# Level differences of three gated recurrences: from the vector engine to GpSimd

## What is computed

```
# gla_mixer (4 heads, dk 64), hgrn2_scan (8 heads, dk 128); b = cumsum(log of the gate)
decay = exp(b[t] - b[s])            for s <= t, else 0
attn  = einsum('td,sd,tsd->ts', q, k, decay)
o     = attn @ v   (+ what the earlier chunks carry in)
```

```
q[t]·k[s]·exp(b[t]-b[s]) = (q[t]·exp(b[t]-b[m])) · (k[s]·exp(-(b[s]-b[m])))     m = the last token of the first half
```

## Time and profile before

| | us |
|---|---|
| median of 3 runs | 1308.67 |
| lowest, highest | 1304.14, 1310.24 |
| the profiled execution, its own time | 1304.06 |
| its span, first to last instruction | 1302.2 |
| PE busy in the span | 1213.9 |
| DVE busy | 794.1 |
| ACT busy | 590.8 |
| POOL busy | 0.2 |

### The profile page before, as it was taken

One profiled execution on the slowest core, in us unless ns is written; L12 is line 12 of the kernel. 1 busy time (PEld: TensorE's weight loads), 2 busy tenths in 40 slices (PEclk: granted clock), 3 DMA queues, 4 the chain that ended last, 5 costly groups with the idle time before them and its releaser, 6 DMA issues. The chain is left out here.

```text
span 1302.2 us, 22187 instructions
## 1 busy us (share of the span) xinstructions
PE 1213.9 (93%) x9296; PEld 1146.4 (88%) x9296; DVE 794.1 (61%) x963; ACT 590.8 (45%) x706; POOL 0.2 (0%) x4
## 2 busy tenths in 40 slices
PE   5999999987999997998988899999999998999997
PEld 4988889987999996898888788888888797999997
DVE  3466666757555556358879544863444665777775
ACT  3553445344443444366444434544333444554553
POOL 0000000000000000000000000000000000000000
PEclk8999899998999998999998899899999899999999
DMA  6522433542555552253222233342333253554540
GB/s 245 194 98 98 162 130 130 195 162 69 190 183 175 190 183 76 79 213 112 102 91 86 98 130 117 110 162 98 130 129 130 97 199 129 184 177 185 190 164 33
DMA packets 26507, 183.14 MB, mean 141 GB/s; under 512 B 3120, under 2 KB 3776, under 8 KB 4544
## 3 DMA queue, kind: packets, MB, share of 16 engines
q1 hardware_dynamic: 26432, 182.04, 39.3%
HBM read 180.98 MB, written 1.05 MB: 140 GB/s over the span
## 5 line engine op out<-in xcount | busy, mean ns | idle before, releaser
L271 DVE TENSOR_TENSOR wlo<-raw,whi 128x2048 fp32r<-128x2048 f32 x170 | 389.4, 2291 | 260.5 <-ACT whi L264 256.9
L276 PE MATMUL pp<-XH,whi 128*128 128x256 f32 x1792 | 516.7, 288 | 11.8 <-DVE HF L811 9.3
L276 PE MATMUL pp<-XL,whi 128*128 128x256 f32 x1792 | 511.5, 285 | 0.0
L276 PE MATMUL pp<-XH,wlo 128*128 128x256 f32 x1792 | 511.2, 285 | 0.0
L276 PEld LDWEIGHTS pp<-XH,whi 128*128 128x128 f32 x1792 | 348.4, 194 | 21.8 <-DVE HF L811 10.6
L264 ACT ACTIVATE whi<-raw 128x2048 fp32r<-128x2048 f32 x170 | 324.0, 1907 | 83.6 <-PE pp L276 61.0
L276 PEld LDWEIGHTS pp<-XL,whi 128*128 128x128 f32 x1792 | 348.7, 195 | 0.0
L276 PEld LDWEIGHTS pp<-XH,wlo 128*128 128x128 f32 x1792 | 348.4, 194 | 0.0
L1326 PE MATMUL pm<-Y,whi 128*128 128x256 f32 x640 | 116.1, 283 | 0.0
L1326 PEld LDWEIGHTS pm<-Y,whi 128*128 128x128 f32 x640 | 99.8, 192 | 0.0
L1326 PE MATMUL pm<-Y,wlo 128*128 128x256 f32 x320 | 90.6, 283 | 0.0
(11 more groups left out here) (278 smaller groups left out, 1384.8 us busy)
## 6 DMA issues: line engine op xcount, KB each, us to landing
raw<-stream SPq DMA_DIRECT2D x170, 1024.0 KB, 4.8
X<-xT SPq DMA_DIRECT2D x1, 1024.0 KB, 4.9
out<-P SPq DMA_DIRECT2D x4, 256.0 KB, 2.4
C<-consts SPq DMA_DIRECT2D x1, 751.5 KB, 12.3
U<-poolw SPq DMA_DIRECT2D x1, 256.0 KB, 11.3
C<-consts SPq DMA_DIRECT2D x1, 192.0 KB, 4.9
PC<-cols SPq DMA_DIRECT2D x1, 189.0 KB, 4.9
P<-masks SPq DMA_DIRECT2D x1, 64.0 KB, 12.0
```

Source lines behind the costliest of these rows:

```text
L271: dve.tensor_tensor(wlo[:, slot, :], raw[:, slot, :], whi[:, slot, :].bitcast(F32), ALU.subtract).then_inc(lo_ready, 1)
L276: done = pe.matmul(dst, a, b, start=first and n == 0, stop=last and n == 2, **kw)
```

## The change

All 24 level differences leave DVE's program and form a program of GpSimd. For each round it waits until the cumulative sums are there (for rounds 1 and 2: of both rounds, `gated_inputs_ready` >= 3), in rounds 1 and 2 also until the scratch use of the same tile in the round before is over (`gated_d_free`, newly raised by L824), and from level 1 on until both exponentials of the level before have read `d`. DVE loses `differences` in all its places; behind L824 it waits for `gated_d_free` in place of its own chain semaphore. ACT, PE and the DMA queue keep their programs, and no work is left out.

```diff
-        if r < 2:
-            differences(0)
         for n in range(8):
             ...
             dve.tensor_tensor(z[:, :, half:], z[:, :, half:], q[:, :, half:], ALU.mult).then_inc(S("gated_z_ready"), 1)
             dve.tensor_tensor(z[:, :, :half], z[:, :, :half], k[:, :, :half], ALU.mult).then_inc(S("gated_z_ready"), 1)
-            if n < 7:
-                differences(n + 1)
...
-        link(dve, dve.scalar_tensor_tensor(o, o, col(g["gain"]), GD(g), ALU.mult, ALU.mult))
-        if r == 1:
-            differences(0, gated(2))
+        dve.scalar_tensor_tensor(o, o, col(g["gain"]), GD(g), ALU.mult, ALU.mult).then_inc(S("gated_d_free"), 1)
+        dve.wait_ge(S("gated_d_free"), r + 1)
...
+    @block.gpsimd
+    def _(pool):
+        for r in range(3):
+            g = gated(r)
+            pool.wait_ge(S("gated_inputs_ready"), 3 if r else 1)
+            if r:
+                pool.wait_ge(S("gated_d_free"), r)
+            for n, half in enumerate(LEVELS):
+                if n:
+                    pool.wait_ge(S("gated_exp"), 2 * (8 * r + n))
+                b, d = blocks(g["b"], half), blocks(g["d"], half)
+                pool.tensor_tensor(d, b, b[:, :, half - 1:half].to_broadcast(list(b.shape)), ALU.subtract)\
+                    .then_inc(S("gated_diff_ready"), 1)
```

## The result

| | before | after |
|---|---|---|
| median, us | 1308.04 (4 runs) | 1318.63 (4 runs) |
| lowest, highest | 1304.14, 1310.24 | 1317.94, 1320.10 |
| ratio | | 1.0086, interval 1.0059 to 1.0112 |
| the profiled execution: time, span | 1304.06, 1302.2 | 1317.94, 1316.1 |

The forecast was 1321 us. The two profiled executions lie 13.9 us apart, the medians 10.6 us, because the profiled execution of before was the lowest of its runs. What follows splits up the 13.9 us of the traces.

What follows compares the result with a forecast made beforehand. PE's idle time was taken as what counts, with round 1 bound by a dependency loop and round 2 by DVE. 10.35 + 0 + 2.8 = +13.2 us gave 1321.9 us against the median, forecast as 1321, range 1301 to 1329.

Steps and rivals of the forecast that it cites:

- What bounds the kernel: PE's idle time counts: round 1 bound by a dependency loop, round 2 by DVE, round 0 by PE except at its ends.
- a ring of 10.6 us: Round 1: pair, score matmuls, exponentials and products each wait for the one before, 10.59 us a turn.
- The wait that replaces the work: Difference on GpSimd and products on DVE, released together, collide reading SBUF; one whole difference per product pair, chance 0.42.
- the upper bound: Each product pair waits one whole GpSimd difference, 2.3 us, rather than 0 with an own read path.
- The price of a difference: On GpSimd a difference takes 2.3 us for 1024 and 1.15 us for 512 elements; far end 3.7 us.
- Round 1: Slower by 10.35 us: 3.45 us before the first products, then three turns growing from 10.6 to 12.9 us.
- The start: Beginning of round 1: difference 1.15 us late behind DVE's split, first products 2.3 us later, together 3.45 us.
- The clock's share: Round 1: PE's longer pauses may each bring a half-clock stretch, 0 to 5 us, in the range only.
- Round 0: Slower by 2.8 us: first difference +0.5, first products +1.15, last waiting products +1.15 us.
- Round 2: Unchanged, 0 us: second and third product pairs give -1.2 us, two turns of 12.9 against 12.3 us give +1.2.
- The sum: Whole kernel: 10.35 + 0 + 2.8 = +13.2 us, PE's slow clock left out.
- The edits said to cost nothing: `gated_d_free`, round 2's first difference behind L824 and the wait for both rounds' sums add no time.

Runs made afterwards that it cites:

- The two placed versions: Kernel before with differences of round 2 alone, or of all rounds, on GpSimd, round 2's beside DVE work reading SBUF once: 1300.24 us and 1302.08 us.
- the additional instruction: Kernel before, differences on DVE, plus seven unused two-input GpSimd instructions in round 1, released by the exponentials: 1316.01 us, ratio 1.0066.
- the copy with one operand: Kernel before, differences on DVE, plus seven unused one-input GpSimd copies of 128x1024 in round 1, released by the exponentials: 1315.19 us, single run.
- the placed version: Kernel before with round 2's differences alone on GpSimd, from level 2 each beside DVE work reading SBUF once: 1300.24 us, ratio 0.9955.

## Why the prediction was right

- *What bounds the kernel.* Right. Round 1 has a ring of 10.6 us and no use for a free DVE; round 2 is bound by DVE before the change. The two placed versions show both: 10.6 us in round 1 whoever computes the differences, and 12.3 down to 10.6 us in round 2.
- *The wait that replaces the work.* Right, and shown alone by the additional instruction. The prediction's rows (693 against 1219 ns of DVE) could not show where GpSimd reads, and it gave this case a chance of 0.42; the choice of the upper bound was no reading of the trace. The prediction let the first product through and GpSimd in behind it. The trace has that once, in the start of round 1 (product 0.69, second product 2.40 us); in the other levels of round 1's ring GpSimd is first by 0.02 to 0.1 us, and the first product waits. The price for the pair of products is the same.
- *The price of a difference.* 1.89 us undisturbed for 1024 elements and 1.04 us for 512, against 2.3 and 1.15 us. For 1024 elements that is 1.8 times the copy with one operand, and less than the split's row. The estimate by the Trainium skill (GPSIMD Engine Reference, Performance versus the Vector engine), also about 2.3 us, is too high here too; the measurement decides.
- *Round 1.* Predicted +10.35 us, measured +12.45. The start, predicted at +3.45 us, is +2.3 us (the pair at 616.54, 8.33 us behind the split, was 5.99 us behind it): the difference is ready 0.6 us late instead of 1.15, and the wait is 1.7 us instead of 2.3. The following three turns, from there to the pair at 657.34, were predicted at +6.9 us and took +8.6 us: 1.7 to 1.8 us of wait each, less than 2.3 us, and the slow clock. The clock's share was given as 0 to 5 us and left out of the sum. The clock's cost is 0.5 us in the first pair of the round and 1.5 us in each of the next three (7.34 for 5.86 us), 4.9 us, at the upper end; the last of these lies behind the turns. So the waits alone would have made about +7.6 us, 2.7 us less than predicted, and the clock, which the sum left out, brought 4.9 us more. That the two errors cancel in part is luck.
- *Round 0.* Predicted +2.8 us, found 2.5 us, again from other parts. The first pair's wait is 2.35 us for 1.01 us, and the last one's 1.76 us for 1.35 us, +0.4 us where +1.15 us was predicted. The missing part is the clock: the first pair takes 8.37 us to its score matmuls (72.48 to 80.85) instead of 7.43 us (71.30 to 78.73), since its slow stretch lasts longer. Its clock is the third number from the end, before and after, from 3 to 6 us behind the pair's start:

```profile
74.30:77.30 3.00, 3.00 (x24) 3.00 (x24) 2.27 (x4) 0.84 (x2) 0.00 (x0) 0.90 0.25 57
```
```profile
75.50:78.50 3.00, 3.00 (x18) 3.00 (x18) 1.56 (x3) 0.00 (x0) 0.00 (x0) 0.58 0.35 55
```
- *Round 2.* Predicted 0 (a start of -1.2 us, turns of 12.9 us), measured -1.2 us with turns of 12.2 to 12.3 us. The start came about as predicted (-1.1 us to the pair at 702.90); the turns have nearly the right length for a wrong reason. The prediction let the ring with a wait set the pace, and said that the split's wait lies in DVE's spare time. The trace shows a DVE without a pause: the exponential ends at 711.94, and the product starts only at 712.67, when DVE has finished the masked copy. In that turn the split is 1.2 us and the product 1.1 us longer, together the 2.3 us that the two differences had taken before. So DVE still bounds round 2, and its own waits are why the turns gain nothing; the placed version removes most of them and reaches the ring's 10.6 us.
- *The sum* of 13.2 us stands against 13.9 us of the two traces and 10.6 us of the medians. So the forecast is right in direction and cause; that it lies within 3 us owes something to luck, with a wait sized too long and a clock left out. The edits said to cost nothing (`gated_d_free`, the wait for both rounds' sums) show no wait of their own: DVE goes on as before, and the difference at 675.36 is long done when its exponential comes (684.89).

## What to carry to other kernels

Before moving an elementwise step off the vector engine, find the ring that sets the pace: in this kernel the move gained only where the vector engine itself was that bound. Then look at what the vector engine runs in the very moment in which GpSimd is released; if both wait on the same semaphore, and both read SBUF with more than one operand on the vector side, the two instructions exclude each other, and one that was off the path is now on it. Here the same 24 differences, released behind the products and in round 2 also beside PSUM-reading work, turned +0.9% into -0.4%; with round 2 alone moved it is -0.5%.

## What the runs showed of the hardware

- A GpSimd instruction that reads SBUF and a DVE instruction with two SBUF inputs run one after the other: product 0.69 to 2.49 us beside a difference of 1.9 us, 0.69 to 1.54 us beside a copy of 1.04 us; split 2.29 to 4.11 us beside an additional difference. In the other direction the first difference of round 1 lasts 4.00 us behind a split. The profile books the wait as busy time of the one that waits, on both engines.
- DVE instructions that read PSUM and one SBUF tensor (masked copy 1.36 us, convolution 2.42 us for six) keep their times beside a GpSimd read, and a GpSimd memset of 128x1024 leaves products at 0.69 us and splits at 2.29 us.
- PE's pauses of 2.6 to 2.8 us in round 1 were followed by a stretch at half the clock (1.2 for 2.4 GHz) in every turn, those of 0.9 to 1.0 us by none. The length of the pause alone does not settle it: in the kernel with GpSimd behind the products, round 2 kept 1.00 behind a pause of 2.54 us and fell to 0.50 behind one of 2.62 us, and with the copies a pause of 1.88 us in round 1 was enough.
